# One projection tile on 32 columns, key norms on 8 columns, and another order of the merged stage

## What is computed

```
gates = jax.nn.sigmoid(proj[..., NSA_WIDTH + 6 * KV_WIDTH:])        # 24 columns: 8 heads x 3 branches
...
kk = heads(k * lp["rwkv_k_k"])
kk = kk / jnp.maximum(jnp.sqrt(jnp.sum(kk * kk, axis=-1, keepdims=True)), 1e-12)
k = k * (1.0 + (a - 1.0) * lp["rwkv_k_a"])
y, s = wkv_scan(rh, heads(decay), kh, vh, -kk, kk * ah, s0)
```

## Time and profile before

| | before |
|---|---|
| median of 3 runs | 1949.68 us |
| profiled execution: its time, its span | 1948.48 us, 1946.5 us |
| instructions in the trace | 53658 |
| PE, PEld busy | 97%, 90% |
| DVE, ACT, POOL busy | 69%, 45%, 4% |
| mean DMA rate | 110 GB/s |
| mean granted clock of PE | 0.989 |

### The profile page before, as it was taken

One profiled execution on the slowest core, in us unless ns is written; L12 is line 12 of the kernel. 1 busy time (PEld: TensorE's weight loads), 2 busy tenths in 40 slices (PEclk: granted clock), 3 DMA queues, 4 the chain that ended last, 5 costly groups with the idle time before them and its releaser, 6 DMA issues.

```text
span 1946.5 us, 53658 instructions
## 1 busy us (share of the span) xinstructions
PE 1884.5 (97%) x22120; PEld 1751.1 (90%) x22120; DVE 1349.7 (69%) x2244; ACT 866.4 (45%) x1694; POOL 72.1 (4%) x143
## 2 busy tenths in 40 slices
PE   7999999998999999999999999999999999999997
PEld 7999888776889999999999998987767999999997
DVE  3485867888647999952255767688886389999423
ACT  3323335554445566652232234445636355666421
POOL 0000000000000111100000000000000001111000
PEclk9999999999999999999999999999999999999999
DMA  6225534234332333233332254442443222332332
GB/s 223 88 76 168 164 110 142 67 111 123 110 97 72 109 99 109 77 99 98 104 139 91 72 182 145 136 130 61 126 137 89 91 98 87 101 107 88 90 96 90
DMA packets 153013, 214.29 MB, mean 110 GB/s; under 512 B 18497, under 2 KB 118338, under 8 KB 151362
## 3 DMA queue, kind: packets, MB, share of 16 engines
q1 hardware_dynamic: 134050, 200.38, 33.2%
q10 hardware_dynamic: 18720, 10.49, 1.8%
HBM read 202.58 MB, written 16.59 MB: 113 GB/s over the span
## 4 chain that ended last, share of the span: by engine, by line
PE 73%; DVE 18%; issue 3%; ACT 2%; DMA 2%; SPq 0%; ACTq 0%; DVEq 0%
PE ps L1119 12%; PE ps L1121 11%; PE ps L1120 11%; PE ps L1666 5%; PE ps L1668 5%; PE ps L1667 5%; PE ps L1520 4%; PE ps L1387 1%; DMA ring<-in_w 1%; PE ps L1491 1%; PE ps L1376 1%; DVE arena L2584 1%; PE ps L1140 1%; PE ps L1141 1%; DVE arena L2593 1%
## 5 line engine op out<-in xcount | busy, mean ns | idle before, releaser
L2260 DVE TENSOR_TENSOR ring_lo<-ring,ring_hi 128x1024 fp32r<-128x1024 f32 x84 | 102.9, 1225 | 198.7 <-ACT ring_hi L1723 196.8
L1121 PE MATMUL ps<-hf_hi,ring_lo 128*128 128x260 f32 x704 | 199.2, 283 | 0.0
L1121 PE MATMUL ps<-in_hi,ring_lo 128*128 128x260 f32 x704 | 199.1, 283 | 0.0
L1723 ACT ACTIVATE ring_hi<-ring 128x1024 fp32r<-128x1024 f32 x84 | 88.9, 1059 | 214.0 <-DMA ring<-in_w 211.1
L1121 PE MATMUL ps<-hm_hi,ring_lo 128*128 128x260 f32 x480 | 137.2, 286 | 0.0
L1121 PEld LDWEIGHTS ps<-hf_hi,ring_lo 128*128 128x128 f32 x704 | 132.9, 189 | 0.0
L1121 PEld LDWEIGHTS ps<-in_hi,ring_lo 128*128 128x128 f32 x704 | 132.8, 189 | 0.0
L1119 PE MATMUL ps<-in_hi,ring_hi 128*128 128x260 f32 x448 | 128.9, 288 | 1.7 <-DVE ring_lo L2260 1.7
L1119 PE MATMUL ps<-hf_hi,ring_hi 128*128 128x260 f32 x448 | 127.7, 285 | 0.3
L1120 PE MATMUL ps<-in_lo,ring_hi 128*128 128x260 f32 x448 | 126.8, 283 | 0.0
L1120 PE MATMUL ps<-hf_lo,ring_hi 128*128 128x260 f32 x448 | 126.8, 283 | 0.0
(11 more groups left out here) (554 smaller groups left out, 6109.3 us busy)
## 6 DMA issues: line engine op xcount, KB each, us to landing
ring<-in_w SPq DMA_DIRECT2D x158, 512.0 KB, 3.5
arena<-in_w SPq DMA_DIRECT2D x44, 512.0 KB, 3.5
extra<-in_kv_cmp SPq DMA_DIRECT2D x96, 128.0 KB, 2.3
arena<-in_kv_cmp SPq DMA_DIRECT2D x80, 128.0 KB, 2.8
slot<-in_kv_cmp SPq DMA_DIRECT2D x80, 128.0 KB, 2.4
out_win_old<-in_win SPq DMA_DIRECT2D x16, 511.0 KB, 4.2
slot<-in_k_sel SPq DMA_DIRECT2D x72, 64.0 KB, 2.1
extra<-in_k_sel SPq DMA_DIRECT2D x72, 64.0 KB, 1.9
```

What stands on the lines that cost most here:

```text
L1121: last = mmul(out, wl, hi[:, k, cols], start=False, stop=(ci == len(chunks) - 1 and at == k1 - 1))
L1723: A(w_high(l, n), w_place(l, n), ACT.Copy).then_inc(S["w_hi"], 1)
L2260: v.tensor_tensor(w_low(l, n), w_place(l, n), w_high(l, n), SUB).then_inc(S["w_lo"], 1)
```

## The change

It has three parts. (1) The gate tile: the 32 first columns of the weight chunk are multiplied in place by the norm's weights (DVE, 128x8x32), and PE multiplies the unsplit input by them in plain fp32, 8 blocks x 4 quarters of 130 tokens, each quarter into its own 32 rows of PSUM. DVE scales the result in 4 instructions of 24x130. The chunk is no longer split. (2) The key norm of every pass: `kknorm` sums into 8 columns; `keymix` has two more instructions on 128x8 (maximum, reciprocal) ahead of its own; `root` works on 128x8 and waits for them; a new step `kspread` on PE spreads the 8 columns over 128x512; `keys` has two instructions left. (3) A new string `ORDER` (745 queued steps for 741).

```diff
@@ rwkv_threads
-        put("root", "ACT", 0.72, *here("kknorm"))
-        put("keys", "DVE", 5.42, *here("root"))
+        put("root", "ACT", 0.35, *here("keymix"))
+        put("kspread", "PE", 1.0, *here("root"))
+        put("keys", "DVE", 1.7, *here("kspread"))
@@ the order of the merged stage
-ORDER = ("700077897880870901788801788071088787087789907088788008887717180088710817071800889177108091071807170898108279788878283338"
+ORDER = ("989070787087988070088081788708008778878877098777888080777987871018710807189870081781870177717180800801787899101710081278"
...
@@ PE
+                def gate_tile():
+                    b = 2 * (dense_n[0] % 3)
+                    pe.wait_ge(S["evac_a"], dense_n[0] - 2)
+                    pe.wait_ge(S["evac_v"], dense_n[0] - 2)
+                    w_wait(NT)
+                    for k in range(KB):
+                        for q, r in enumerate(QROWS):
+                            last = mmul(ps[r, b, 0:TQ], gate_weights(l)[:, k, :], x[:, k, q * TQ:(q + 1) * TQ], start=(k == 0), stop=(k == KB - 1))
+                    last.then_inc(S["w_used"], 1)
+                    dense_n[0] += 1
...
-                        mmul(ps[:, 3, :], blk, t0, start=True, stop=True).then_inc(T["kk1"], 1)
+                        for j in range(RJ):
+                            last = mmul(ps[:, 3, 2 * j:2 * j + 2], t0[:, j, :], blk[:, 0:P:HD], start=True, stop=True)
+                        last.then_inc(T["kk1"], 1)
+                    elif stage == "kspread":
+                        pe.wait_ge(*at_sc("root1", 1))
+                        for j in range(RJ):
+                            for h, r in enumerate(HP):
+                                last = mmul(ps[r, 3, j * SC:(j + 1) * SC], kinv[:, 2 * j + h:2 * j + h + 1].to_broadcast((P, HD)), ident, start=True, stop=True)
+                        last.then_inc(T["kk1"], 1)
@@ PE, mean of the pass before
-                            pe.wait_ge(*at_sc("root1", 2))
+                            pe.wait_ge(*at_sc("prep", 3))
@@ ACT
-                        if l + n // N_CHUNK < DEPTH:
+                        if l + n // N_CHUNK < DEPTH and n != NT:
...
-                        act.wait_ge(*at_sc("kk1", 1))
-                        o.go(A(t1, b4(3), ACT.Sqrt))
+                        act.wait_ge(kk_rec, l * (LAST_SC + 1) + sc + 1)
+                        o.go(A(kinv, kinv, ACT.Sqrt))
@@ DVE
+                        if n == NT:
+                            dve.wait_ge(*w_landed(l, n))
+                            v.tensor_tensor(gate_weights(l), gate_weights(l), wide(C("mix_pre"), QR), MUL).then_inc(S["w_lo"], 1)
...
-                        evac_scaled(gate_rows[0:24, :], 24)
+                        dve.wait_ge(S["w_used"], tile_done(NT))
+                        for q in range(4):
+                            to, r = slice(q * TQ, (q + 1) * TQ), slice(QR * q, QR * q + 24)
+                            o.go(v.tensor_tensor(gate_rows[0:24, to], ps[r, 2 * (NT % 3), 0:TQ], rs[r, to], MUL))
+                        o.tell(S["evac_v"])
+                        n_dense[0] += 1
...
+                        o.do(v.tensor_scalar(kinv, ps[:, 3, 0:2 * RJ], 1e-24, None, MAX))
+                        o.do(v.reciprocal(kinv, kinv))
+                        dve.sem_inc(kk_rec, 1)
                         o.go(v.tensor_tensor(km, cc, x_sc[:, RJ:2 * RJ, :], MUL))
                     elif stage == "keys":
-                        dve.wait_ge(*at_sc("root1", 1))
-                        bounded(o, kk, t1, aa, bb)
+                        dve.wait_ge(*at_sc("kk1", 2))
+                        o.do(v.tensor_tensor(kk, kk, b4(3), MUL))
+                        o.go(v.scalar_tensor_tensor(bb, aa, 1.0, kk, ADD, MUL))
```

More of the change, by code:

```diff
@@ L425, in warm_thread @@
     return [(("warm", i, "ones"), "PE", 0.9, [att[-2][0]]) for i in range(WARM)]
-ORDER = ("700077897880870901788801788071088787087789907088788008887717180088710817071800889177108091071807170898108279788878283338"
-         "283227782288327288782727827977788278277883389227838282383887121789782178227977728288327718727882827817878891177188882812"
-         "218728978227217872183722892128872271728872787887287828274787882422487243878882842747988888973732227892732888233787827334"
-         "273828837282871238777228712887372778178178927162217821789172217788278811729872728722812277781278281272282822776827872847"
-         "493242846782824272326982273727367237924232738722742378231971727392371112277682121772728121971712211977262722782618728732"
-         "822928227288272782782882778262987224872868447822822722882996976824773272672772747823297633272878272327972376872277829234"
-         "772272274272222723727332273722764477874548447475873874888")
+ORDER = ("989070787087988070087781088708008778878877098777888080777987871018710807189870081781870177717180800801787899101710081278"
+         "783232783733223882382288388777217823122227827782389287728782388872178818977228128727782727278171819272817128871828872711"
+         "829288789188887778728122228278788292878222737272388778878827792784788922278822787288478224287488287788274823838729782772"
+         "328788782473824727983782323788287133287193817812721112827822883111228779822881278876827288122872182772276812487874871829"
+         "978464877782422332226672739272232277392342782378672377224772171322398717326981122721772721791221187228217677298178812778"
+         "222887722281812788228227477464282782287222696982877842287222796732287287722972877864987227823377233726272727737282473232"
+         "7722722427272279232233723226274474794987677488374874487855787")
 def merged_order():
@@ L557, in w_place, with gate_weights @@
             return apart_raw if n == C_UP + 2 else ring[:, (N_CHUNK * l + n) % RING, :]
+        def gate_weights(l):
+            return w_place(l, NT).rearrange("p (k m) -> p k m", k=KB)[:, :, 0:QR]
         def w_high(l, n):
@@ L620, in build @@
         km, piv = t0, cum
+        kinv = t1.rearrange("p j t -> p (j t)")[:, 0:2 * RJ]
         vtm = at(2, RJ, CH)
@@ L837, in build @@
         gate_in, val_in = x_ok[0:2], x_ok[2:5]
+        kk_rec = ctx.enter_context(nc.semaphore("kk_rec"))
         const_ok = ctx.enter_context(nc.semaphore("const_ok"))
@@ L1242, in _ @@
                 for m in range(FRONT, N_IN):
+                    if m == NT:
+                        gate_tile()
+                        continue
                     dense_tile([(m, 0, KB)], in_hi, in_lo)
@@ L1358, in rwkv @@
                             pe.wait_ge(*at_sc("prep", 2))
-                            pe.wait_ge(*at_sc("root1", 1))
                             if sc:
@@ L2507, in rwkv @@
                     elif stage == "rkv":
-                        dve.wait_ge(*at_sc("kk1", 2))
+                        dve.wait_ge(*at_sc("kk1", 3))
                         o.go(v.tensor_tensor(rk, b4(3), y, MUL))
```

4 lines of the change are left out of this document (2 added, 2 removed).

## The result

The changed kernel takes 1965.57 us (median of 8 runs, 1960.22 to 1969.18) against 1951.45 us (median of 8, 1947.93 to 1954.69): a ratio of 1.0072, 95% interval 1.0061 to 1.0084. It is slower by 14 us. I had said 1947.0, within 0.3% as the likeliest case, and a range that ended at 1957. The profiled execution has a span of 1966.3 us, 19.8 more than before. A profile shows one execution only; this one took 1968.13 us, 2.6 more than the median.

What follows compares the result with a forecast made beforehand. PE, busy 1884.5 of 1946.5 us, was taken as the bound. Terms -7.0 + 7.5 - 4.0 + 1.4 - 2.0 + 4.5 - 2.0 = -1.6 us gave a forecast of 1947.0 us, range 1938 to 1957.

Steps and rivals of the forecast that it cites:

- waits ahead of `pairb`: Merged stage, passes 0 and 2: PE's waits for DVE's `scaled` would go as DVE sheds 3.3 us, -4 us.
- The term for the order elsewhere: Remaining short PE waits in the merged stages, shifted by the new order: -2 us, useful ends -10 to +8, unpriced.
- rival 2: Slower by the clock: two more half-clock stretches of 6.8 us per layer, +12.4 us, 1959 us; chance 0.20.
- the 0.47 that I had priced: Share of a half-clock stretch taken as lost, from 13 products busy 2.86 us instead of 1.53 us.
- Key norm, PE: Every pass: wide sum of 1.05 us replaced by narrow sum 0.99 and spread 1.02 us, +7.5 us in all.
- the variant of rival 1: Key norm's narrow sum costs PE next to nothing, 6.4 us less, 1940.6 us; chance 0.04.
- rival 1: Faster: DVE was the hidden bound of the merged stages, -7 us on the sum, 1940 us; chance 0.34.
- The wait that I had feared at `mean`: Passes 1 and 3: `mean` waits for the next pass's finished keys, sharing a PSUM bank; +1.4 us.
- Gate tile: PE's gate tile falls from 5.7 to 1.9 us per layer, less 0.3 us of wait: -7.0 us.
- Rival 3: Gate tile gives nothing: PE waits behind it for the next chunk's split or Tanh, 1954 us; chance 0.08.
- the 0.5 that I had allowed: Sign for the gate tile: no PE idle over 0.5 us in the two tiles behind it.
- Head and end of the stage: Merged stage: head waits of 1.05 and 0.88 us covered, -2 us; `wlo` on the end's path, +4.5 us.

Runs made afterwards that it cites:

- e17_act3: Kernel before with the gate tile alone, ACT issuing 3 of 16 selected pages per unit instead of 4, SP 13: 1949.40 us, ratio 0.9990.
- e2_key: Kernel before with the key norm change alone, old order with the spread put half way between root and keys: 1969.43 us, ratio 1.0103.
- e3_gate_key: Kernel before with gate tile and key norm changes, old order plus the spread steps: 1959.17 us, ratio 1.0046.
- e1_gate: Kernel before with the gate tile change alone, key norm and order as before: 1948.12 us, ratio 0.9992.
- e4_order: Kernel before with the new order alone, without the spread steps: 1976.39 us, ratio 1.0147.
- e15_wide_tail: e1_gate with three unused products of 128x512 among thin steps and two more in the gap at the merged stage's end: 1952.54 us, ratio 1.0014.

## Why the prediction was wrong

Two steps failed. I put the clock at nothing in the sum, where the runs showed 20 us more at half clock per layer, and I let the waits ahead of `pairb` go for -4 us, where that of pass 0 grew by 2.5 and 2.0 us. The term for the order elsewhere, -2 us, had no row behind it; the new order costs 5 to 6 us with both edits in place and 27 us alone.

**The clock, rival 2, was named rightly and believed too little.** I gave two more stretches of 6.8 us per layer 0.20 and called a time of 1959. There are some 20 us more at half clock per layer, and each us of it cost less than the 0.47 that I had priced: within the two merged stages 37 us more at half clock stand beside 8.5 us more of PE's busy time than the new work explains, 0.23 us each. The gap at the end of the stage, which `wlo` and the order nearly doubled, is one cause: filling it took the stretch behind it away each time, some 3 us for two layers by the profiles, 6.3 by the medians. The stretch is no fixed price of the gap: behind the same wait of 2.46 us it was 3.4 us long in the kernel before and 6.8 in layer 1 of `e17_act3`. Widening the narrow sum, whose 2 columns I had valued only by their time, gave 4.4 and 3.7 us, but the rows show no stretch that begins at it. Long waits for pages and for the late transfer have stretches behind them as well. In my sum all this stood as work and links alone. My argument against it, a mean clock of 0.98 in spite of many short products, hid that the kernel before already ran 14 us per stage at half clock.

**Key norm, PE.** The spread came as worked out, 1.03 us, and the narrow sum near it, 0.81 to 1.16 us. As a price of the work the term of +7.5 us stands; as a price of the edit it fails, for alone the edit costs 20 us. The row decided rightly against a price of 0.2 us, and the variant of rival 1 that rests on it is out.

**The waits ahead of `pairb`.** "With 3.3 us less of DVE these go" held in the old order (`e2_key`, `e3_gate_key`) and failed in the new one. The step that failed is that I took DVE's own work as the only thing ahead of `scaled`. `scaled` also waits for the sample's state to be stored, and the new order issues that store 4.7 us later in the stage. I had not followed `scaled`'s second wait. Instead of -2 us for pass 0 the wait grew by 2.5 and 2.0 us, and without the transfer the kernel is 8.2 us faster. In pass 2 the wait hardly changed (0.52 and 0.28 us). The wait that I had feared at `mean`, +1.4 us, is 0.13 us, in one layer.

**Gate tile.** The tile itself is right (1.9 us, -3.5 us in the input stage). Rival 3's worry about splits and Tanh is out in layer 1, where PE waits 0.17 us for the gates behind it; in layer 2 it waits 0.73 us, more than the 0.5 that I had allowed, and the dense stage with the input tiles gained 1.7 us of 3.5. Alone the edit gave 1.6 us of 7. In `e1_gate` ACT issued the pages of the second unit 281.8 us into the stage and those of its values at 309.6, where the kernel before has 281.1 and 307.8, and the four issues for the unit of keys ahead took 2.76 us, those for the values 2.69, instead of 1.82; PE got to the second unit's keys 0.5 us earlier. No term of mine held that, and what delayed the issues is not shown.

**Head and end of the stage.** The waits of 1.05 and 0.88 us are gone, as said. The end came at 4.61 us against 4 to 5 forecast.

**DVE as a hidden bound, rival 1,** is refuted: 13.7 us of DVE per layer went and PE's idle time grew. In the old order too it stayed where it was (`e2_key`, 16.1 and 16.2 us).

**What is open.** PE's busy time and the half clock don't fit one price. In `e2_key` the 13.2 us more at half clock of layer 1 stand beside 5.7 us of busy time that is not new work, 0.43 us each. At that price the 18.3 us of the changed kernel's layer 1 would be 7.9 us, while its busy time rose by 4.6 beyond the work. So either the new order saves some 3 us of short pipeline gaps per layer, or its stretches fall where they cost less; `e4_order` has the same difference (1.7 us more busy beside 13.3 us more at half clock in layer 1), and no run parts the two. What starts the two stretches near 5 and 46 us into the stage, which all kernels have (only layer 1 of `e15_wide_tail` lacks the second), is open as well. The second comes without a wait. In the 10 us ahead of it, in the kernel before, PE was busy and at full clock:

```profile
208.00:218.20 10.20, 10.15 (x179) 9.26 (x178) 7.27 (x18) 6.03 (x18) 0.00 (x0) 1.00 0.75 220
```

## What to carry to other kernels

Where a kernel is held by PE, give each edit two prices, its time and what it leaves of PE's activity: a gap costs more than its own length when the clock falls behind it, and half clock can come behind short products without a gap. Here 128 columns in place of 2 cost 0.1 us per sum and saved 4 us in all, which only a run could tell. Before a step is called unblocked by a shorter predecessor, read every wait that stands in front of it, the stores that must leave its buffer first among them. And test one part at a time: here three parts of -2, +20 and +27 us make +14 together.
